# One early down tile in each of twelve pairs instead of two in six, and the tables' digits and iota made in the mixer

## The reference

```python
q = (ht @ w_q).reshape(T, PEER_HEADS, PEER_QDIM)
s1 = einsum('thd,kd->thk', q[..., :PEER_HALF], keys_1)
s2 = einsum('thd,kd->thk', q[..., PEER_HALF:], keys_2)
v1, i1 = top_k(s1, 16); v2, i2 = top_k(s2, 16)
cand = v1[..., :, None] + v2[..., None, :]          # 256 candidates
vals, ci = top_k(cand, 16)
e_idx = i1[ci // 16] * 128 + i2[ci % 16]
gates = softmax(vals)
# per token, over its 128 experts
act = gelu(h . expert_down[e_idx])
y = sum(gates * act * expert_up[e_idx])
```

## Time and profile before

| | |
|---|---|
| timed runs | 2771.34, 2771.84, 2774.01 us |
| profiled execution | 2768.73 us, its span 2766.9 us |
| TensorE busy | 2691.1 us, 97% |
| VectorE busy | 2211.4 us, 80% |
| GpSimd busy | 1990.7 us, 72% |
| ScalarE busy | 885.6 us, 32% |
| DMA | 717.78 MB |
| mean granted TensorE clock | 0.994 |

### The profile page before, as it was taken

The page is one execution under the profiler, slowest core; times in us unless marked ns, Lnnn a source line. Parts: engine busy times, 40 slices in busy tenths (PEclk is TensorE's granted clock), DMA queues, the critical chain, the costliest instruction groups (busy, mean ns, idle before and its releaser), DMA issues.

```text
span 2766.9 us, 40220 instructions
## 1 busy us (share of the span) xinstructions
PE 2691.1 (97%) x14885; PEld 2371.8 (86%) x14885; DVE 2211.4 (80%) x4772; ACT 885.6 (32%) x1511; POOL 1990.7 (72%) x1505
## 2 busy tenths in 40 slices
PE   8999999999998999999999999999999999999997
PEld 6788787787898989899989988998899889988996
DVE  2522788654998968888988998888889989889998
ACT  4422444324324652222222222222222322222222
POOL 5543577674886877777777868776877687768774
PEclk9999999999999999999999999999999999999999
DMA  4233422234235999899989989998999899989995
GB/s 158 68 93 107 160 70 85 77 99 140 77 104 195 278 311 328 329 345 345 346 333 335 355 323 346 344 346 316 344 348 339 313 363 353 344 311 358 342 345 204
DMA packets 267730, 717.78 MB, mean 259 GB/s; under 512 B 20880, under 2 KB 104208, under 8 KB 267536
## 3 DMA queue, kind: packets, MB, share of 16 engines
q0 software_dynamic: 110912, 403.75, 38.7%
q1 hardware_dynamic: 156624, 311.48, 33.5%
HBM read 657.73 MB, written 57.41 MB: 258 GB/s over the span
## 4 chain that ended last, share of the span: by engine, by line
PE 45%; DVE 7%; DMA 6%; POOL 4%; issue 1%; ACT 1%; DVEq 0%; SPq 0%; ACTq 0%; POOLq 0%
PE abank L1934 8%; PE abank L1936 8%; PE abank L1935 8%; PE ybank L1950 7%; PE ybank L1949 7%; PE ybank L1951 7%; DMA up<-in_up,e_idx 2%; DMA up<-in_down,e_idx 2%; DVE acc L2111 2%; DVE up L2099 2%; POOL tdown_lo L1881 2%; DVE e_y L2185 1%; POOL up L1874 1%; DMA w<-all_pre 1%; POOL tup_lo L1885 1%
## 5 line engine op out<-in xcount | busy, mean ns | idle before, releaser
L1934 PE MATMUL abank<-m_hT,tdown_hi 128*128 128x384 f32 (+1 forms) x1856 | 578.3, 312 | 14.6 <-DVE w_lo L2177 8.7
L1936 PE MATMUL abank<-m_hT,tdown_lo 128*128 128x384 f32 (+1 forms) x1856 | 577.7, 311 | 0.0
L1935 PE MATMUL abank<-m_hlo,tdown_hi 128*128 128x384 f32 (+1 forms) x1856 | 576.8, 311 | 0.0
L2111 DVE SCALAR_TENSOR_TENSOR acc<-up,e_act,acc 128x1024 f32<-128x1024 f32 x381 | 489.4, 1284 | 68.8 <-DMA up<-in_up,e_idx 51.2
L2099 DVE CUSTOM_DVE_ANT_0 up<-up,acc 128x1024 f32<-128x1024 f32 x384 | 455.1, 1215 | 82.5 <-DMA up<-in_down,e_idx 82.0
L1949 PE MATMUL ybank<-tup_hi,w_hi 128*128 128x512 f32 x1280 | 502.8, 393 | 12.0 <-DVE w_lo L2177 9.5
L1021 POOL TENSOR_TENSOR m_wlo<-m_raw,m_whi 128x1024 fp32r<-128x1024 f32 x128 | 311.6, 2439 | 265.1 <-ACT m_whi L791 261.3
L1950 PE MATMUL ybank<-tup_lo,w_hi 128*128 128x512 f32 x1280 | 501.5, 392 | 0.0
L1951 PE MATMUL ybank<-tup_hi,w_lo 128*128 128x512 f32 x1280 | 501.1, 392 | 0.0
L1874 POOL DMA_INDIRECT up<-in_down,e_idx x384 | 364.4, 949 | 98.7 <-issue 77.1
L1874 POOL DMA_INDIRECT up<-in_up,e_idx x384 | 363.4, 946 | 98.9 <-issue 74.4
(11 more groups left out here) (279 smaller groups left out, 4169.7 us busy)
## 6 DMA issues: line engine op xcount, KB each, us to landing
e_tup<-in_up SPq DMA_DIRECT2D x128, 512.0 KB, 5.6
m_raw<-in_tiles SPq DMA_DIRECT2D x116, 512.0 KB, 3.5
e_tdown<-in_downT SPq DMA_DIRECT2D x116, 512.0 KB, 5.3
gates<-all_table SPq DMA_DIRECT2D x64, 640.0 KB, 4.2
all_table<-t_out SPq DMA_DIRECT2D x9, 4096.0 KB, 14.4
m_raw<-in_downT SPq DMA_DIRECT2D x12, 512.0 KB, 3.7
up<-in_down,e_idx POOLq DMA_INDIRECT x384, 6.6
up<-in_up,e_idx POOLq DMA_INDIRECT x384, 6.5
```

The costliest lines, as they stand in the source:

```text
L1934: nc.tensor.matmul(out, tdown_hi[:, q, at], h2T_hi[:, k, a:b], start=k == 0, stop=False)
L1935: nc.tensor.matmul(out, tdown_hi[:, q, at], h2T_lo[:, a:b, at], start=False, stop=False)
L1936: ins = nc.tensor.matmul(out, tdown_lo[:, q, at], h2T_hi[:, k, a:b], start=False, stop=k == KD - 1)
L2111: ins = nc.vector.scalar_tensor_tensor(out=acc[:], in0=src, scalar=act_of[:, b, k:k + 1], in1=acc[:], op0=ALU.mult, op1=ALU.add)
```

## The change

Early tiles are now `PRE = [(p, 1) for p in range(4, NPAIR, 5)]`: tile q = 1 of pairs 4, 9, 14, ... 59, twelve in all. Before it was both tiles of pairs 4, 14, ... 54, twelve too. `SHARE` gives the pairs ahead of them 12 where an ordinary pair has 20, which is 8 rows (once 7). ScalarE makes the high part of (p+2, 1) directly behind that of (p+2, 0) where (p+1, 1) is early, and SyncE loads an early tile first in the order of the pair before that. In the mixer the first keys are transposed between the halves of the last early product, copied by ScalarE right away, and made into digits by VectorE; iota goes to PSUM there too. VectorE makes its last choice of first keys ahead of the gates' start.

```diff
-PRE = list(range(4, NPAIR, 10))
-NPRE = 2 * len(PRE)
+PRE = [(p, 1) for p in range(4, NPAIR, 5)]
+NPRE = len(PRE)
...
                 for half, (a, b) in enumerate(SPLIT):
+                    if half and i == NPRE - 1:
+                        pe.wait_ge(lead_in, 64)
+                        pe.wait_ge(pre_kept, NPRE - 2)
+                        pe.wait_ge(chosen, NG * PH - 1)
+                        pe.wait_ge(last_chosen, 1)
+                        turn_cols(0, sel_all[:, 0])
...
+            pe.wait_ge(pre_kept, NPRE - 1)
+            pe.wait_ge(last_chosen, 2)
+            turn_cols(2, sel_all[:, 1])
+            pe.wait_ge(sel_kept, 2)
+            pe.wait_ge(topk_done, NG)
+            turn_cols(1, gate_all[:])
...
             for i in range(NPRE):
                 if i == NPRE - 1:
+                    keep_cols(0, 0)
                     gates_exp(NG - 1)
...
+            keep_cols(2, 2)
+            act.wait_ge(pre_kept, NPRE)
+            nc.scalar.activation(banks[ROH][:, 0:P], const[:, C_IOTA:C_IOTA + P], ACT.Copy)
+            keep_cols(1, 4)
...
+            last_choice(0)
             gates_start()
-            last_choice(0)
+            last_choice(1)
             gates_end(NG - 1)
-            last_choice(1)
+            dve.wait_ge(sel_kept, 2)
+            link(nc.vector.tensor_scalar(digits[:, 1], cols[:, 0], 0.5 - LOWS / 2, TO_LOWS, ALU.add, ALU.add))
+            link(nc.vector.tensor_scalar(digits[:, 0], digits[:, 1], TO_LOWS, None, ALU.subtract))
+            nc.vector.tensor_tensor(digits[:, 1], cols[:, 0], digits[:, 0], ALU.subtract)
...
-            nc.scalar.activation(iota, const[:, C_IOTA:C_IOTA + P], ACT.Copy).then_inc(iota_ready, 1)
...
-            dve.wait_ge(iota_ready, 1)
-            digits_of(slice(0, TQ))
             hots_of_digits(0)
             for u in range(NQUAD):
                 s, t = u // QG, u % QG * 4
-                if u == 2:
-                    digits_of(slice(TQ, DT))
...
-SHARE = [3 if p + 1 in PRE or p + 1 == NPAIR else 10 if p else 6 for p in range(NPAIR)]
+SHARE = [12 if (p + 1, 1) in PRE else 6 if p + 1 == NPAIR else 20 if p else 12 for p in range(NPAIR)]
...
             for p in range(NPAIR):
+                if (p + 2, 1) in PRE:
+                    load_pre(PRE.index((p + 2, 1)))
                 if p + 2 < NPAIR:
                     load_tdown(p + 2, 1)
...
-                if p + 2 in PRE:
-                    for q in range(2):
-                        load_pre(p + 2, q)
...
             def down_half(p, q, half):
-                if p in PRE:
+                if (p, q) in PRE:
                     return
...
                 if p + 2 < NPAIR:
                     down_high_of(p + 2, 0)
+                    if (p + 1, 1) in PRE:
+                        down_high_of(p + 2, 1)
                 up_high_of(p + 1, 1)
...
-                if p + 2 < NPAIR:
+                if p + 2 < NPAIR and (p + 1, 1) not in PRE:
                     down_high_of(p + 2, 1)
```

More of the change, by code:

```diff
@@ L272, in mixer @@
         cols = place("cols", [P, 3, DT], F32, at_cols)
+        digits = place("digits", [P, 2, DT], F32, at_cols + 4 * 3 * DT)
         pre = place("pre", [P, 2, DT], F32, at_q)
@@ L750, in _, with turn_cols @@
                 pe.wait_ge(qd_ready, g * 2 * PH + 2 * PH)
+            def turn_cols(of, src):
+                for t in range(ND):
+                    ins = nc.tensor.transpose(turned_to(of)[t // 4][:, t % 4 * P:(t % 4 + 1) * P], src[:, t], ident)
+                    if t in (3, ND - 1):
+                        ins.then_inc(sel_turned, 1)
             pe.wait_ge(lead_low, 1)
@@ L1464 @@
 QG, QV = 10, 5
+ROH = 4
+TO_LOWS = LOWS * 1.5 * 2.0 ** 23
 TQ, TV = 4 * QG, 4 * QV
@@ L1732, in places_of_experts, with normal, normal_of, halves_of @@
     return late
-def normal(p):
-    return p - sum(n < p for n in PRE)
+def normal(p, q=0):
+    return 2 * p + q - sum(n < (p, q) for n in PRE)
+def normal_of(p, q):
+    return p - sum(n < p and of == q for n, of in PRE)
+def halves_of(n, half=1):
+    return 2 * n + half + 1
 def halves(p, q, half=1):
@@ L1797, in load_tdown, with load_pre @@
             def load_tdown(p, q):
-                if p in PRE:
+                if (p, q) in PRE:
                     return
-                sp.wait_ge(down_low, 2 * (normal(p) - 1) + q + 1)
+                before = max(n for n in range(p) if (n, q) not in PRE)
+                sp.wait_ge(down_low, normal(before, q) + 1)
                 sp.dma_start(tdown[:, q], io["downT"][2 * p + q]).then_inc(tdown_in[q], 16)
-            def load_pre(p, q):
-                read = PRE.index(p) and PRE[PRE.index(p) - 1]
-                sp.wait_ge(gl_ready if read else w_low, halves(read, q))
-                sp.dma_start(w[:, q], scr["pre"][2 * PRE.index(p) + q]).then_inc(pre_in[q], 16)
+            def load_pre(i):
+                if i >= 2:
+                    sp.wait_ge(gl_ready, halves(*PRE[i - 2]))
+                else:
+                    sp.wait_ge(w_low, halves(0, i % 2))
+                sp.dma_start(w[:, i % 2], scr["pre"][i]).then_inc(pre_in[i % 2], 16)
             def load_tup(p, q):
@@ L1968, in down_high_of @@
             def down_high_of(p, q):
-                if p in PRE:
+                if (p, q) in PRE:
                     return
-                act.wait_ge(tdown_in[q], 16 * (normal(p) + 1))
+                act.wait_ge(tdown_in[q], 16 * (normal_of(p, q) + 1))
                 if p:
-                    act.wait_ge(a_ready, halves(normal(p) - 1, q))
+                    before = max(n for n in range(p) if (n, q) not in PRE)
+                    act.wait_ge(a_ready, halves_of(normal(before, q)))
                 nc.scalar.activation(tdown_hi[:, q], tdown[:, q], ACT.Copy).then_inc(down_high, 1)
```

67 lines of the change are left out of this document (23 added, 44 removed).

## The result

| | before | after |
|---|---|---|
| timed, median (lowest to highest) | 2771.59 us (2769.14 to 2774.01) | 2808.61 us (2808.43 to 2810.10) |
| profiled execution, its span | 2768.73 us, 2766.9 us | 2808.68 us, 2806.7 us |
| mean granted TensorE clock | 0.994 | 0.984 |

The ratio after to before is 1.0141, with a 95% interval from 1.0128 to 1.0153: the change costs 37 us. The forecast was 2802.5.

The account below looks back on a forecast made before the run. TensorE, busy 97% of the span, was taken as the bound. 2768.7 - 27.8 (old waits) + 61.2 (new waits and clock) - 2.7 (tables) = 2799.4, plus 3.1 for the median: 2802.5 us, range 2774 to 2820.

Parts of the forecast that it names:

- The old waits go, -27.8: Expert stage: all TensorE waits around the six old early pairs vanish, -27.8 us.
- The fifth product waits for the addition behind the row of f, 3.6 a pair: Pairs 3, 8, ... 58: fifth up product waits for VectorE's addition of product 2, 3.6 us (3.1 to 4.3).
- The clock, 1.5 a pair: Behind each such wait TensorE's clock falls to half for 3.4 us, costing 1.5 us a pair (0 to 3.4).
- The rival in which the clock holds: New pairs: wait as forecast but clock stays at 2.4 GHz, 43.2 instead of 61.2 us, 2784.5; chance 0.21.
- Nothing late behind it: Pair behind each new pair: nothing late, VectorE some 1.7 us behind, second tdown_lo ready early.
- the rival of a sequel: Pair behind each new pair is late too, 12 x 1.8 = 21.6 us more, 2824; chance 0.12.
- The early high part costs nothing: ScalarE's early high part of tdown, the next pair's q = 1, only stands behind the one that counts.
- The tables, -2.7: Mixer's end and table stage: two runs of digits gone, -0.9 and -1.8 us; 4.5 gained if the clock returns sooner.
- The sum: Whole kernel: 2768.7 - 27.8 + 61.2 - 2.7 = 2799.4 us profiled, 2802.5 with 3.1 for the median.
- The low end of my own case: Whole kernel: no clock loss, 12 waits of 3.1 us and -4.5 at the tables, 2776.6 us.

Follow-up runs that it names:

- gather_first: Changed kernel, but in the twelve pairs ahead of an early tile GpSimd issues third- and fourth-part gathers before the low part; 2760.68 us, ratio 0.9973.
- add_first: Changed kernel, but in the twelve pairs ahead of an early tile VectorE adds product 2 before the row of part f; 2779.32 us, ratio 1.0035.
- experts_alone: Kernel before, with only the new early tiles, SHARE and loop over pairs; 2807.54 us, ratio 1.0140.
- high_late: Changed kernel, but ScalarE makes the high part of (p+2, 1) at the end of the pair again; 2804.65 us, ratio 1.0134.
- repeat_product: Changed kernel, but TensorE does the fourth up product twice in the twelve pairs ahead of an early tile; 2787.95 us, ratio 1.0076.
- all_three: Changed kernel with late gathers before the low part, product 2 added before f's row, high part of (p+2, 1) at pair's end; 2748.16 us, ratio 0.9920.
- gather_high_late: gather_first, but ScalarE makes the high part of (p+2, 1) at the end of the pair again; 2750.70 us, ratio 0.9931.
- tables_alone: Kernel before, with only the new end of the mixer and new digits of the table stage; 2766.76 us, ratio 0.9994.

## Why the prediction was right, step by step

- **The old waits go, -27.8.** Right: no wait for `w_lo` is left around early tiles (one of 0.64 us ahead of pair 43 comes from the late pair 42), and each pair behind takes 27.9 us. Waits at other places grew by 2.8 us, most of it in pair 21 (3.1 over an ordinary pair, before 1.9) and pair 42.
- **The fifth product waits for the addition behind the row of f, 3.6 a pair.** Right, in place, in reason and nearly in size. It is 3.75 on average (45.0 / 12), and the steps of pair 23 are within 0.1 us of the forecast. The landing I had taken from the earlier trace rows, 5.67 us; in pair 23 it was 1688.65 - 1682.96 = 5.69, and 5.4 to 6.1 in the eleven pairs in which VectorE waited for that row. In pair 43 the row was there when VectorE, itself late, came to it. gather_first shows that GpSimd's order is the cause. add_first shows that VectorE's order has a part in it: changed alone it takes away 29 us, and the late row costs the rest elsewhere.
- **The clock, 1.5 a pair.** The term that was too small: (68.9 - 45.0) / 12 = 2.0. I had taken 3.4 us of the lower clock, with one wait in ten without it. It fell in all twelve pairs. Where it fell for 3.4 us it cost 1.4 to 1.7, about what I had put down. In five pairs it fell for 6.8 us and cost 2.3 to 2.8, and this length had shown once and I had left out of the size. In experts_alone and high_late, with waits of 2.6 to 4.5 us, the mean was 1.7. repeat_product shows that it hangs on the idle time. The rival in which the clock holds is refuted for this kernel. The Trainium skill (TensorE: Matmul & The Clock Gate, HAM oscillation — how this bites in real kernels) tells of a loop in which every wait for data brings the clock down. The traces agree for 33 of the 36 waits of these three profiles, and not for the other three.
- **Nothing late behind it.** Right: no wait in the next pair, and the rival of a sequel is refuted for this kernel. It came to life in add_first and all_three, where the wait no longer held TensorE back.
- **The early high part costs nothing.** Wrong, at one place above all. I had counted what it stands behind, and not that its load may be late: in pair 43, where SyncE's loads were late, ScalarE waited 3.92 us for it in the changed kernel, and 5.87 in gather_first. In the changed kernel it was covered for the most part by the other wait (4.8 us there), in gather_first it cost about 8 us. In ten of the other pairs of gather_first it cost 0.4 us each, as gather_high_late shows.
- **The tables, -2.7.** The size came out, its parts did not. The 0.9 us ahead of the first quad don't show: from VectorE's choice to the first quad it takes 12.8 us where it took 12.4. The stage behind it is 2.7 us shorter between the two halves of the change, and 3.7 between the kernels before and after (153.5 and 149.8). The idle time of 1.43 is gone, and the clock comes back sooner (0.83 and 0.72 instead of 0.50 and 0.57 in the same stretch), which I had named as possible and not counted. So the match with 2.7 is in part luck. The first up product of pair 1 came 3.9 us earlier, in the ten profiles with the new tables 2.1 to 4.2; but in experts_alone, with the old ones, it came 1.2 earlier too. In the whole time it is not resolved.
- **The sum.** 68.9 instead of 61.2 and 2.8 of other waits, less 1.2 more gained at the tables, make the profiled execution 9.3 us longer than the 2799.4 forecast. The 3.1 us that I added for the difference of median and profiled execution didn't come again (2808.61 and 2808.68), so the forecast is 6.1 us low. (The low end of my own case adds up to 2776.7, not 2776.6, which changes nothing.)

What stays open: why some waits of 2 to 4 us leave the clock alone and others don't, what the tables' part is worth in the whole, and why pairs 21 and 42, where a block of tokens ends, take 1.1 to 4.1 us more in every kernel with the new loop.

## What to carry to other kernels

When work is taken out of a bottleneck engine's stretch, list for each engine that serves it what is queued behind its longest wait there. If transfers are issued behind a wait that they don't need, the memory can run dry, as it did here for 3.1 us. Here moving two gathers ahead of one wait was worth 48 us, more than the change had cost. An edit that makes something "early" on an in-order engine has to be priced by the latest arrival of its input, at the worst place of the loop, and not by the usual one.

## What the runs showed of the hardware

The length of a wait doesn't say alone whether the clock falls. In high_late a wait of 2.78 us in pair 23 left the clock at 2.4 GHz, and one of 2.64 in pair 28 brought it down. The first matmuls behind each (idle times 2.62 and 2.48 in brackets), and the stretches of 7 us around them:

```profile
1689.90 0.50 PE L1967 MATMUL ybank<-tup_hi,w_hi 128*128 128x512 f32 x1 [2.62 <-DVE e_y L2205]
...
1825.04 0.79 PE L1967 MATMUL ybank<-tup_hi,w_hi 128*128 128x512 f32 x1 [2.48 <-DVE e_y L2205]
```

```profile
1685.00:1692.00 7.00, 4.38 (x20) 3.27 (x19) 4.63 (x11) 1.74 (x3) 6.50 (x5) 1.00 0.86 304
...
1820.00:1827.00 7.00, 4.52 (x17) 3.36 (x16) 4.78 (x11) 1.74 (x3) 6.51 (x5) 0.86 0.90 317
```

In experts_alone one of 3.85 us (pair 53) left it alone, too. The waits of 0.7 to 1.1 us at the fifth product of gather_first never brought it down. In between both happened. In tables_alone the clock fell behind idle times of 1.91, 2.02 and 2.29 us (the prediction's 1.78 of the kernel before had left it alone), and held behind one of 2.62. The first and the last of these four, with the stretches behind them:

```profile
1144.12 0.36 PE L1940 MATMUL abank<-m_hT,tdown_hi 128*128 128x256 f32 x1 [1.91 <-DVE w_lo L2183]
...
2200.44 0.50 PE L1955 MATMUL ybank<-tup_hi,w_hi 128*128 128x512 f32 x1 [2.62 <-DVE w_lo L2183]
```

```profile
1144.50:1147.80 3.30, 3.30 (x17) 3.30 (x17) 3.30 (x8) 0.00 (x0) 3.13 (x2) 0.50 1.01 375
...
2200.00:2204.00 4.00, 3.56 (x16) 2.94 (x17) 1.57 (x3) 0.23 (x2) 3.35 (x2) 1.00 0.90 261
```
